# Building one-hot operands for expert gates: pairs of tokens innermost

## What is computed

```python
def block(xb):
    q = (xb @ w_q).reshape(PEER_TOKEN_BLOCK, PEER_HEADS, 2, PEER_HALF)
    s = jnp.einsum('thcd,hckd->thck', q, sub_keys).astype(jnp.float32)
    s1, i1 = lax.top_k(s[:, :, 0], PEER_TOPK)
    s2, i2 = lax.top_k(s[:, :, 1], PEER_TOPK)
    cand_s = (s1[..., :, None] + s2[..., None, :]).reshape(PEER_TOKEN_BLOCK, PEER_HEADS, PEER_TOPK * PEER_TOPK)
    cand_i = (i1[..., :, None] * PEER_NKEYS + i2[..., None, :]).reshape(PEER_TOKEN_BLOCK, PEER_HEADS, PEER_TOPK * PEER_TOPK)
    top_s, pos = lax.top_k(cand_s, PEER_TOPK)
    eidx = jnp.take_along_axis(cand_i, pos, axis=-1)
    gate = jax.nn.softmax(top_s, axis=-1).astype(xb.dtype)
    h = jax.nn.gelu(jnp.einsum('thkd,td->thk', u[eidx], xb), approximate=False)
    return jnp.einsum('thk,thkd->td', gate * h, v[eidx])
```

## Time and profile before

| | us |
|---|---|
| median of 3 runs | 2657.28 (2650.49 to 2660.39) |
| the profiled execution's own time | 2657.64 |
| its span in the trace | 2655.8 |

### The profile page before, as it was taken

The page is one execution under the profiler, slowest core; times in us unless marked ns, Lnnn a source line. Parts: engine busy times, 40 slices in busy tenths (PEclk is TensorE's granted clock), DMA queues, the critical chain, the costliest instruction groups (busy, mean ns, idle before and its releaser), DMA issues.

```text
span 2655.8 us, 41584 instructions
## 1 busy us (share of the span) xinstructions
PE 2486.7 (94%) x16494; PEld 2251.4 (85%) x16494; DVE 2003.6 (75%) x3049; ACT 1107.5 (42%) x1660; POOL 296.8 (11%) x124
## 2 busy tenths in 40 slices
PE   7998999999999999789998999999999688998999
PEld 7877998999988888578998999988888577787987
DVE  6577797999967766768897999876676657556675
ACT  3341344444454555120444444445545253333333
POOL 0000496000000000000694000000000102000000
PEclk9999999999999999889999999999999799899999
DMA  6544676666677777424676666777777441233545
GB/s 218 175 131 139 193 215 192 187 181 188 196 246 261 231 245 242 144 80 142 191 204 195 182 187 183 211 247 252 242 243 238 119 133 40 70 125 124 168 149 175
DMA packets 201425, 483.65 MB, mean 182 GB/s; under 512 B 24080, under 2 KB 93712, under 8 KB 200720
## 3 DMA queue, kind: packets, MB, share of 16 engines
q1 hardware_dynamic: 197632, 472.42, 57.5%
q10 hardware_dynamic: 3600, 8.57, 0.9%
HBM read 446.30 MB, written 34.60 MB: 181 GB/s over the span
## 4 chain that ended last, share of the span: by engine, by line
PE 57%; DVE 30%; POOL 5%; DMA 4%; ACT 3%; issue 2%; ACTq 0%; DVEq 0%; SPq 0%
PE psum L1036 26%; PE psum L812 19%; DVE rounded L1483 9%; DVE halves L2418 8%; DVE halves L2415 5%; PE psum L989 5%; POOL rounded L785 5%; DMA sb<-in_u_turned 2%; PE psum L1147 1%; ACT rounded L2836 1%; DVE rounded L1479 1%; ACT rounded L2500 1%; DVE sb L1518 1%; DVE sb L2290 1%; PE psum L970 1%
## 5 line engine op out<-in xcount | busy, mean ns | idle before, releaser
L1483 DVE TENSOR_TENSOR rounded<-sb,rounded 128x1024 fp32r<-128x1024 f32 (+3 forms) x696 | 813.4, 1174 | 408.4 <-ACT rounded L2836 231.2
L2836 ACT ACTIVATE rounded<-sb 128x1024 fp32r<-128x1024 f32 x512 | 542.7, 1060 | 787.6 <-PE psum L1036 327.5
L989 PE MATMUL psum<-rounded 128*128 128x256 f32 x6144 | 773.7, 285 | 14.1 <-POOL rounded L785 14.0
L989 PEld LDWEIGHTS psum<-rounded 128*128 128x128 f32 x6144 | 746.8, 192 | 17.7 <-POOL rounded L785 17.6
L1036 PE MATMUL psum<-rounded,weights 128*128 128x512 f32 x3072 | 697.5, 389 | 1.7 <-DVE weights L2427 1.3
L1036 PEld LDWEIGHTS psum<-rounded,weights 128*128 128x128 f32 x3072 | 576.3, 188 | 122.3 <-issue 2.9
L812 PE MATMUL psum<-rounded 128*128 128x256 f32 (+1 forms) x3924 | 600.4, 315 | 41.4 <-DVE rounded L1483 32.8
L812 PEld LDWEIGHTS psum<-rounded 128*128 128x128 f32 x3924 | 550.0, 197 | 88.9 <-DVE rounded L1483 27.3
L2500 ACT ACTIVATE rounded<-sb 128x1024 fp32r<-128x1024 f32 (+2 forms) x222 | 206.7, 942 | 327.5 <-PE psum L812 204.7
L785 POOL TENSOR_TENSOR rounded<-sb,rounded 128x1024 fp32r<-128x1024 f32 x96 | 268.6, 2813 | 483.7 <-ACT rounded L2836 483.0
L2418 DVE TENSOR_TENSOR halves<-halves,small 128x1536 bf16<-128x1536 bf16 x128 | 225.0, 1758 | 4.4
(11 more groups left out here) (368 smaller groups left out, 1533.3 us busy)
## 6 DMA issues: line engine op xcount, KB each, us to landing
sb<-in_u_turned SPq DMA_DIRECT2D x256, 512.0 KB, 4.0
sb<-in_peer_v SPq DMA_DIRECT2D x256, 512.0 KB, 3.5
hidden<-sb SPq DMA_DIRECT2D x256, 128.0 KB, 4.0
sb<-hidden SPq DMA_DIRECT2D x256, 128.0 KB, 3.5
sb<-in_ret_w_in SPq DMA_DIRECT2D x48, 512.0 KB, 3.9
sb<-in_ffn_w_up SPq DMA_DIRECT2D x40, 512.0 KB, 4.0
sb<-in_peer_w_q SPq DMA_DIRECT2D x32, 512.0 KB, 3.8
sb<-in_ffn_w_down SPq DMA_DIRECT2D x22, 512.0 KB, 4.2
```

The source lines that it names most:

```text
L989: mm = pe.matmul(ps(bank, 1)[:, 0:T], u[p][:, k * P:(k + 1) * P], hT[:, q, k, :], start=(k == 0 and w == 0), stop=(k == KD - 1 and w == 2))
L1483: vec.tensor_tensor(ring_lo[0:k, part, 0:wide], ring[0:k, slot, 0:wide], ring_hi[0:k, part, 0:wide].bitcast(F32), ALU.subtract).then_inc(c ...
L2836: act.activation(ring_hi[:, n % SPLIT, :], ring[:, n % RING, :], ACT.Copy).then_inc(tile_hi, 1)
```

## The change

The one instruction that made both one-hots of a group becomes two. The one for i writes its four tokens as two pairs, with the two tokens of a pair side by side for each of the 128 values of i; it compares a new table `iota_two` (each number twice in a row) with the two tokens' i. The one for j keeps its layout and writes 128 values in a row for each token. The multiplication by the gate parts becomes two instructions, one for each pair, in the same paired layout. TensorE reads the gated one-hot of one token as every second element. `iota_two` lies in a free piece of `misc` and is written once in each phase.

```diff
@@
+        misc_at = lasting.at
@@
-        gate_onehot = half_parts.take(2, 3, 4, P)
+        gate_onehot = half_parts.take(2, 3, 2, P, 2)
@@
+        doubled = nc.alloc_sbuf_tensor_at("doubled", [P, 2 * P], BF16, offset=SB_AT + 4 * (misc_at + 276))
+        iota_two = Memory(doubled, 0, 2 * P).take(P, 2)
@@
-                                           gate_onehot[:, buf, p, q, :], start=(q == 0 and p == 0), stop=(p == 2),
+                                           gate_onehot[:, buf, p, q // 2, :, q % 2], start=(q == 0 and p == 0), stop=(p == 2),
@@
                 vec.tensor_copy(iota_half, iota).then_inc(*own.next())
+                vec.tensor_copy(iota_two, bcast(iota, 2, 2)).then_inc(*own.next())
@@
-                    vec.tensor_tensor(ij_onehot[:, buf], bcast(bcast(iota_half, 1, 4), 1, 2), bcast(routes[:, 0:2, t], 3, P),
+                    i_pairs = ij_onehot[:, buf, 0].rearrange("p a b -> p (a b)").rearrange("p (q c two) -> p q c two", q=2, two=2)
+                    of_pair = routes[:, 0, t].rearrange("p (q two) -> p q two", two=2)
+                    vec.tensor_tensor(i_pairs, bcast(iota_two, 1, 2), bcast(of_pair, 2, P), ALU.is_equal).then_inc(*own.next())
+                    vec.tensor_tensor(ij_onehot[:, buf, 1], bcast(iota_half, 1, 4), bcast(routes[:, 1, t], 2, P),
                                       ALU.is_equal).then_inc(*own.next())
                     done()
-                    vec.tensor_tensor(gate_onehot[:, buf], bcast(ij_onehot[:, buf, 0], 1, 3), bcast(routes[:, 2:5, t], 3, P),
-                                      ALU.mult).then_inc(*own.mark(onehots_made))
+                    for q in range(2):
+                        pair = slice(4 * g + 2 * q, 4 * g + 2 * q + 2)
+                        vec.tensor_tensor(gate_onehot[:, buf, :, q], bcast(i_pairs[:, q], 1, 3), bcast(routes[:, 2:5, pair], 2, P),
+                                          ALU.mult).then_inc(*(own.mark(onehots_made) if q else own.next()))
```

## The result

The changed kernel takes 2639.95 us in the median of 6 runs (2636.74 to 2642.45), the kernel before 2657.47 in the median of 6 (2650.49 to 2661.44). The ratio is 0.9942, with a 95% interval of 0.9931 to 0.9954: 0.58% faster, 15.4 us by the ratio and 17.5 by the medians. The profiled execution took 2636.74 us, with a span of 2634.9.

What follows compares the result with a forecast made beforehand. VectorE was taken as the bound, TensorE close behind. From 2657.64 us, two layers of 7.6 (steady stretch) and 0.95 (first group) came off and 0.7 (clock) was added: -16.4, so 2641 us; 8-in-10 range 2635 to 2663.

Steps and rivals of the forecast that it cites:

- The bound: In the stretch with the groups, VectorE ends last; TensorE, close behind, takes over once VectorE's step is under 3.96 us.
- The rate: VectorE's i one-hot and products go at two elements a tick, j at one; a group's step falls from 4.06 to 3.10 us.
- The steady stretch: From group 0 to group 63 on TensorE, 269.67 us falls to 262.1, a gain of 7.6 us in each layer.
- the read with a step of 4 bytes: TensorE's streamed gate operand was forecast to cost nothing more when read 4 bytes apart; upper bound 20 us.
- The first group: Ahead of group 0, the group is ready 2.06 us behind its start, not 3.02: 0.95 us gained in each layer.
- The clock: Behind group 0 in layer 0, TensorE's half clock after idling comes to light and costs 0.7 us.
- The half rate of TensorE's reads: Rival: TensorE's reads of every second element cost half the rate, 81 us, giving 2722 us; chance 0.06.
- Pairs without the upper rate: Rival: VectorE's paired instructions stay at one element a tick, 14 us more, giving 2672 us; chance 0.07.

Runs made afterwards that it cites:

- e4: The changed kernel with one product of each group made twice on VectorE; 2642.52 us, ratio 0.9962 to the kernel before.
- e2: The changed kernel with the two products walking the same bytes token by token; 2657.62 us, ratio 1.0016 to the kernel before.
- e1: The changed kernel with i's one-hot made from a table that repeats each number by a step of zero; 2639.32 us, ratio 0.9946 to the kernel before.
- e6: The changed kernel with TensorE reading its 128 gate columns in a row, so the output is wrong; 2641.04 us.
- e11: The changed kernel once more, unaltered, in another batch; 2638.28 us, ratio 0.9938 to the kernel before.
- e7: The changed kernel with all four tokens innermost, one product instruction a group and TensorE reading every fourth element; 2723.46 us, ratio 1.0248 to the kernel before.
- e3: The kernel before with a group's work cut into four instructions, but in the old layout; 2673.52 us, ratio 1.0067 to the kernel before.
- e10: The changed kernel with TensorE reading every third element, 6 bytes apart, so the output is wrong; 2676.78 us in one run.
- e9: The changed kernel with TensorE reading every eighth element, 16 bytes apart, so the output is wrong; 2996.36 us, ratio 1.1289 to the kernel before.

## Why the prediction was right, step by step

**The bound.** VectorE ended last and TensorE was close behind; that the gain stops at TensorE's pace was right, and the knee between e4 and e2 shows it. VectorE's busy time fell by 107 us (2003.6 to 1896.4) and the stretch of the groups by 15.

**The rate.** Products 555 ns (forecast 553), i 419 (418), j 685 (693), the step 3.13 us (3.10). The bounds were drawn by rows and the upper rate was unseen in them; the rule of the Trainium skill, "Vector Engine (DVE) Microarchitecture Reference", section 5.1, had it, and the trace of the changed kernel agrees: with two neighbours innermost, 768 elements in 555 ns and 512 in 419 are 1.9 to 2.0 elements a ns beyond the fixed 0.16 us, and with an innermost step of zero 512 in 685 are half of that. e1 shows it for i alone, 684 ns without the neighbours and 419 with them (from 460 to 700 us of e1):

```profile
L2421 DVE TENSOR_TENSOR halves<-small 128x512 bf16<-128x512 bf16 x57 | 39.0, 684 | 0.0
```

**The steady stretch.** 6.6 us a layer against 7.6. The term that I had taken at nothing, the read with a step of 4 bytes, is 0.013 us on a group, and 63 of them make up the difference but for 0.1: 263.04 and not 262.1, by e6.

**The first group.** It was ready 2.06 us behind its start by the forecast; in the trace 446.23 to 448.32, 2.09. From the first tile behind the transposes to the second half the changed kernel takes 288.46 and 288.69 us, the kernel before 734.69 - 438.68 = 296.01 in layer 0 and 296.27 in layer 1. Both layers together are 15.1 us, some 13.2 from the steady stretch and 1.9 ahead of group 0.

**The clock.** The 0.7 us that I had added did not appear: no step behind group 0 was slow in the changed kernel or in e11 (3.63 us at once). In layer 0 of e4, with 2.01 us of idle time ahead of group 0 in place of 1.41, it did appear:

```profile
449.20:453.00 3.80, 3.80 (x28) 3.80 (x27) 3.73 (x7) 0.60 (x1) 0.00 (x0) 0.59 0.43 110
```

There the first step is 5.12 us and not 3.63, and that is why e4's span of the groups is 264.53. What brings it about is open. The idle time alone does not settle it: layer 1 of the kernel before idled 2.60 us without it, and so did layer 1 of e4 with 2.01; e7 idled only 1.34 and 1.35 and had it in both layers. TensorE's timeline in e7, the tiles behind groups 0 and 1:

```profile
450.24 4.61 PE L992 MATMUL psum<-rounded 128*128 128x256 f32 x24
...
455.99 3.13 PE L992 MATMUL psum<-rounded 128*128 128x256 f32 x24
```

**The rest.** The two profiled executions differ by 20.9 us in span, and the groups explain 15.1. Most of the rest lies where no instruction was changed. The two windows begin 1.7 us into the second half of layer 1, from 1706.04 us of the span after and 1720.56 before (columns of the earlier trace rows):

```profile
1706.04:2634.90 928.86, 853.22 (x4716) 744.02 (x4716) 601.25 (x929) 393.44 (x593) 26.00 (x22) 0.96 0.53 168
```

```profile
1720.56:2655.80 935.24, 860.81 (x4716) 751.59 (x4716) 601.56 (x929) 393.82 (x593) 25.54 (x22) 0.95 0.52 167
```

They are 928.86 us at a clock of 0.96 and 935.24 at 0.95; the same kernel again (e11) needed 933.89. The matmuls of that second half take 348.4 us in both, so the difference lies behind it. So that part moves by 5 us from one execution to the next, and 15 us is what the change is worth; the 15.4 of the ratio agree. Against the 16.4 of the forecast that is 1.3 less, from two errors that in part cancel: 2.0 us too much for the steady stretch, and 0.7 for a clock effect that did not come. That 2641 lies 1 us from the median of 2639.95 is in part luck: the medians differ by 17.5 us and the traces account for 15.1.

**The rivals.** The half rate of TensorE's reads did not come at 4 bytes, but it exists: e7 shows it at 8, at about the price that the rival had (81 us forecast, 83 measured). The rule cited with it, "SBUF — State Buffer" of the Trainium skill, section "Door 1: The DMA port swizzle" (full bandwidth while two accesses fall in one 16-byte line), holds at 4 bytes and fails at 8, where two accesses do fall in one line and the rate is half. Pairs without the upper rate would have been 2672; e3 measured 2674 for that, with the old layout.

## What to carry to other kernels

Two engines that are both some 99% busy are bound by the later one only down to the pace of the other, so work out that pace first. Here, by the limit of 3.98 us, 0.1 us of the 0.93 saved a group would be enough for the gain between the groups. That was not measured so close to the limit; e4, which saves 0.33, keeps 12 of the 15 us. In these two-source bf16 instructions one operand that repeats a number by a step of zero innermost held VectorE at about one element a ns, and two neighbours innermost were enough to double it. Two is also the most that TensorE's streamed operand bore here without a price that counts; four neighbours saved VectorE nothing that counted and cost 83 us.

## What the runs showed of the hardware that was not expected

A bf16 operand streamed by TensorE takes 54, 57, 82, 108 and 211 ns for 128 columns at steps of 2, 4, 6, 8 and 16 bytes (e6, the changed kernel, e10, e7, e9). VectorE's product of 768 bf16 elements takes 955 ns with neighbours in a row and an innermost step of zero on one input, and 1059 ns when the output and the other input have a step of two elements (1006 to 1082 over its 256 instructions); why the step costs 0.1 us there was not followed.
